# Feed-forward stages of a two-block transformer kernel: h's high and low parts in one 512-column product, halves added by VectorE

## The chip, the core and the metric

One Trainium2 chip, of which the program uses one core. The metric is the device time of one execution in microseconds (us); the table below has three runs. Names used: PE is TensorE, ACT is ScalarE, DVE is VectorE, POOL is GpSimd, SP is SyncE, whose queue issues the weight loads.

## The reference, cut to what matters

256 tokens of 1024 features pass six stages in float32: a gated MLP mixer, a feed-forward stage, an attention mixer, a second feed-forward stage, a gated linear attention mixer (GLA), and a convolutional feed-forward stage. Both plain feed-forward stages are

```python
h = modulate(rms_norm(x, norm_g[layer, 2]), sh2, sc2)               # 256 x 1024
y = jnp.square(jax.nn.relu(h @ ff_w_in[layer])) @ ff_w_out[layer]   # 1024 -> 4096 -> 1024
x = x + g2[:, None, :] * rms_norm(y, norm_g[layer, 3])
```

and the last stage is `u, gate = split(h @ w_up)`, a 3x3 convolution of `u` over a 4x64 grid, then `(silu(u) * gate) @ w_down` (1024 -> 2 x 2816 -> 1024). The modulation vectors (`sh`, `sc`, `g`) come from products of a condition vector with large matrices (`ada_w`), which are spread over the stages.

## The kernel before, in words

**Two-part products.** Each float32 factor is split into a high part (rounded to the matmul type, `fp32r`) and a low part (the rest). A product is the sum of three: high x high, high x low, low x high. For a weight chunk of 1 MB (a tile of 128 x 2048) ACT copies the raw tile to `whi` (L705, `hi`) and DVE writes `wlo = raw - whi` (L1174, `lo`). There are 6 raw slots and 3 slots of whi/wlo (`SPL`): `hi(m)` waits until PE has multiplied chunk m-3, `lo(m)` waits for `hi(m)`, PE waits for `lo(m)`. `hcat[:, kt, 0, :]` is the high part hh of the stage's input, `hcat[:, kt, 1, :]` the low part hl, each 256 tokens wide and side by side.

**A feed-forward stage** goes over 16 chunks c of 256 hidden features. PE's order is: ff_in(c+1), then rows(c). `ff_in(c)` (`linear_mid`, then `feature_major`) is 2 tiles of 128 features x 8 slices of h x 3 products of 256 columns (L1891 whi with hh, L1892 whi with hl, L1893 wlo with hh), 48 matmuls, all into one PSUM bank. `rows(c)` (`rows_onto_y`, L1959) multiplies the squares `fhi`, `flo` of chunk c (stationary) with the 512-column halves of the output weights, 24 matmuls. PSUM banks of ff_in rotate over 6, 4, 5.

**The step between them** (`epi(c)` in both `ffn` functions): ACT takes the relu out of PSUM to `fr` (L840) when ff_in(c) is done, then squares it into `fm` (L844); DVE squares `fr` into `fhi` (L1447) and subtracts, `flo = fm - fhi` (L1450). All 512 columns wide. Every engine runs its own list in program order. After epi(c), ACT does hi for the weights of rows(c) and of ff_in(c+2); DVE does lo for rows(c), then the condition products (next paragraph), then lo for ff_in(c+2).

**Condition products.** `FF_ADA[f][c]` says how many 1 MB chunks of ada_w are loaded and used at chunk c: 2,2,1,2,1,2,1,2,1,2,1,2,1,2,2,0 in the first stage, 2 and then fourteen 1 in the second. DVE multiplies and adds them (L1206 for 2048 columns; L1199 and L1202, a pair for a gate chunk); a batch of them ends with four matmuls that sum over the partitions (L1815) and its first one waits for the sum of the last batch of its kind.

**Other places that the change touches.** `oP` is the start of a region of the on-chip memory that each stage uses anew; `fhi`, `flo` and, in the last stage, `chi`, `clo` (the same parts of the gated activations, L1767 and L1772) lie in it. `GAIN_BANKS` names the PSUM banks for the gain rows (L1835). In attention, `rows_onto_y(M_BO[0])` is the first output product (two tiles of 128 tokens) and stands between head pair 7's two turns. In the last stage's last chunk, DVE does 4 of 8 convolution taps (L1755), lo of the last weight chunk, the other taps, waits for ACT's silu, then L1767, waits for ACT's `chi`, then L1772.

## Time and profile before

| what | value |
|---|---|
| median of 3 runs | 1033.72 us (1033.54 to 1035.16) |
| the profiled execution | 1034.27 us |
| its span, first to last instruction | 1032.5 us |
| granted TensorE clock, mean | 0.998 |
| PE matmul busy | 1005.6 us, 97% |
| DVE busy | 798.3 us, 77% |
| ACT busy | 537.9 us, 52% |
| HBM read | 239.37 MB |

The busy time of PE counts pipelined matmuls that overlap: a matmul of 256 columns is shown with 0.28 us, but the next one starts 0.12 us after it. What a matmul costs is read from the distance of the starts. The span's 1032.5 us leave 1.8 us of the profiled execution outside.

### The profile page before, as it was taken

To read this page: it belongs to the slowest core of one execution; us is meant where nothing else is said; L and a number is where in the kernel's file an instruction comes from. 1 tells how busy PE (TensorE), PEld (TensorE's weight loads), DVE (VectorE), ACT (ScalarE), POOL (GpSimd) and SP (SyncE) were. 2 spreads that over 40 slices of the span, in tenths; PEclk is the share of its full clock that TensorE was granted. 3 is DMA by queue.
4 is the path that set the end of the run, shared out by engine and by line. 5 is a ranking of instruction groups with operands and counts; after the bars stand their busy time and mean duration, and the time that the engine had idled before them with its cause. 6 is when DMAs were issued, how large, how long until landed. Compare 5 with 4: busy or idle time off the path is not lost.

```text
span 1032.5 us, 17024 instructions
## 1 busy us (share of the span) xinstructions
PE 1005.6 (97%) x6953; PEld 882.6 (85%) x6953; DVE 798.3 (77%) x1196; ACT 537.9 (52%) x706; POOL 76.2 (7%) x80
## 2 busy tenths in 40 slices
PE   6999999999999999999999999999999999999996
PEld 3687799888888999887989899898998789999995
DVE  2458798777988987867968778872796889878896
ACT  4353644445446457765545444455764565454543
POOL 0000000000000000000720000000890000000000
PEclk9999999999999999999999999999999999999999
DMA  9998699887997998003988787724344185656501
GB/s 340 387 391 334 232 339 360 310 333 263 357 327 258 287 369 317 2 2 124 391 305 322 260 289 281 245 78 136 124 163 160 46 285 205 199 169 203 167 39 42
DMA packets 130333, 243.62 MB, mean 236 GB/s; under 512 B 6586, under 2 KB 95311, under 8 KB 124111
## 3 DMA queue, kind: packets, MB, share of 16 engines
q1 hardware_dynamic: 125616, 238.77, 65.7%
q10 hardware_dynamic: 4639, 3.76, 1.3%
q8 instruction: 55, 0.90, 0.4%
q14 instruction: 23, 0.19, 0.1%
HBM read 239.37 MB, written 1.05 MB: 233 GB/s over the span
## 4 chain that ended last, share of the span: by engine, by line
PE 74%; DVE 11%; DMA 5%; SPq 3%; ACT 3%; issue 3%; DVEq 0%; ACTq 0%
PE bank L1959 21%; PE bank L1891 12%; PE bank L1893 12%; PE bank L1892 12%; DVE wlo L1174 3%; DMA raw<-in_a_w_in_dram 3%; SPq L635 2%; PE bank L1971 2%; PE bank L2244 1%; DMA raw<-in_b_w_in_dram 1%; PE bank L1847 1%; PE bank L1797 1%; PE bank L2270 1%; DMA raw<-in_ff_w_in_dram 1%; ACT whi L705 1%
## 5 line engine op out<-in xcount | busy, mean ns | idle before, releaser
L1174 DVE TENSOR_TENSOR wlo<-raw,whi 128x2048 fp32r<-128x2048 f32 x144 | 330.9, 2304 | 51.6 <-ACT whi L705 50.6
L705 ACT ACTIVATE whi<-raw 128x2048 fp32r<-128x2048 f32 x144 | 274.1, 1904 | 146.2 <-PE bank L1959 80.4
L1891 PE MATMUL bank<-hcat,whi 128*128 128x256 f32 x1096 | 312.5, 285 | 1.1 <-DVE wlo L1174 1.1
L1893 PE MATMUL bank<-hcat,wlo 128*128 128x256 f32 x1096 | 309.9, 283 | 0.0
L1892 PE MATMUL bank<-hcat,whi 128*128 128x256 f32 x1096 | 309.9, 283 | 0.0
L1891 PEld LDWEIGHTS bank<-hcat,whi 128*128 128x128 f32 x1096 | 209.8, 191 | 7.7 <-issue 3.0
L1892 PEld LDWEIGHTS bank<-hcat,whi 128*128 128x128 f32 x1096 | 209.9, 192 | 1.5
L1893 PEld LDWEIGHTS bank<-hcat,wlo 128*128 128x128 f32 x1096 | 209.9, 192 | 0.0
L1755 DVE SCALAR_TENSOR_TENSOR cvt<-ut,vec,cvt 128x189 f32<-128x189 f32 (+2 forms) x176 | 68.1, 429 | 21.0 <-ACT cvt L1137 18.6
L1959 PE MATMUL bank<-whi,fhi 128*128 128x512 f32 x240 | 76.5, 400 | 0.0
L1959 PE MATMUL bank<-whi,flo 128*128 128x512 f32 x240 | 75.4, 395 | 0.0
L1959 PE MATMUL bank<-wlo,fhi 128*128 128x512 f32 x240 | 74.9, 393 | 0.0
L840 ACT ACTIVATE fr<-bank 128x512 f32<-128x512 f32 x32 | 19.1, 598 | 90.6 <-PE bank L1893 84.5
L1206 DVE SCALAR_TENSOR_TENSOR acc_wide<-raw,csil,acc_wide 128x2048 f32<-128x2048 f32 x28 | 65.6, 2342 | 0.6
L1959 PEld LDWEIGHTS bank<-wlo,fhi 128*128 128x128 f32 x240 | 45.2, 188 | 10.8
L1959 PEld LDWEIGHTS bank<-whi,flo 128*128 128x128 f32 x240 | 45.0, 188 | 10.4
L1959 PEld LDWEIGHTS bank<-whi,fhi 128*128 128x128 f32 x240 | 43.3, 189 | 11.5 <-issue 3.4
L1447 DVE TENSOR_TENSOR fhi<-fr 128x512 fp32r<-128x512 f32 x32 | 22.4, 698 | 27.5 <-ACT fr L840 27.0
L1797 PE MATMUL bank<-raw,cpad 128*32 128x512 f32 x256 | 32.7, 627 | 6.5 <-DMA raw<-in_ada_w_dram 5.2
L786 ACT ACTIVATE t<-bank,mod,coef 128x256 f32<-128x256 f32 x64 | 30.4, 577 | 8.8 <-PE bank L1847 8.8
L1959 PE MATMUL bank<-whi,hcat 128*128 128x512 f32 x112 | 32.0, 394 | 1.4 <-DVE hcat L1734 1.4
L717 ACT ACTIVATE stage<-bank 128x512 f32<-128x512 f32 x15 | 9.1, 608 | 41.3 <-PE bank L1815 26.3
(425 smaller groups left out, 1651.1 us busy)
## 6 DMA issues: line engine op xcount, KB each, us to landing
raw<-in_ada_w_dram SPq DMA_DIRECT2D x40, 1024.0 KB, 8.3
raw<-in_ff_w_in_dram SPq DMA_DIRECT2D x32, 1024.0 KB, 7.2
raw<-in_ff_w_out_dram SPq DMA_DIRECT2D x32, 1024.0 KB, 6.9
raw<-in_w_ada_dram SPq DMA_DIRECT2D x24, 1024.0 KB, 6.2
raw<-in_w_up_dram SPq DMA_DIRECT2D x22, 1024.0 KB, 5.0
raw<-in_w_in_dram SPq DMA_DIRECT2D x12, 1024.0 KB, 5.4
raw<-in_w_down_dram SPq DMA_DIRECT2D x11, 1024.0 KB, 4.9
raw<-in_ada_w_dram SPq DMA_DIRECT2D x16, 512.0 KB, 12.2
```

Of the source, the lines that this page charges most:

```text
L635: sp.dma_start(raw[:, n % RAW, 0:k * w].rearrange("p (k n) -> p k n", n=w), s)\
L705: act.activation(whi[:, m % SPL, 0:w], raw[:, pl.nm[m] % RAW, 0:w], ACT.Copy).then_inc(s_hi, 1)
L786: act.activation(t32[:, kt, :], ps[banks[kt // 2]][:, T * (kt % 2):T * (kt % 2) + T], ACT.Identity, scale=coef[:, c, kt:kt + 1], bias=mod[ ...
L1174: dve.tensor_tensor(wlo[:, m % SPL, 0:w], raw[:, pl.nm[m] % RAW, 0:w], whi[:, m % SPL, 0:w], ALU.subtract).then_inc(s_lo, 1)
L1206: ins = dve.scalar_tensor_tensor(out=to[:, :], in0=w, scalar=s, in1=to[:, :], op0=ALU.mult, op1=ALU.add)
L1447: dve.tensor_tensor(fhi[:, c % 3, :], fr[:, :], fr[:, :], ALU.mult).then_inc(s_fh, 1)
L1755: ins = dve.scalar_tensor_tensor(out=y, in0=grid(ut)[:, frm[0], frm[1]], scalar=vec[:, w_:w_ + 1], in1=y, op0=ALU.mult, op1=ALU.add)
L1797: mm = pe.matmul(ps[ADA_BANK][32 * g:32 * g + 32, :], cpad[:, c, k, :], w, start=i == 0, stop=i == CHUNKS[b] - 1)
L1891: pe.matmul(dst, wh[:, kt, n], ah[:, kt, :], start=kt == 0, stop=False)
L1892: pe.matmul(dst, wh[:, kt, n], al[:, kt, :], start=False, stop=False)
L1893: mm = pe.matmul(dst, wl[:, kt, n], ah[:, kt, :], start=False, stop=kt == KT - 1)
L1959: mm = pe.matmul(ps[2 * t + half][:, :], st_, w[:, k, n[half]], start=first and k + i == 0, stop=False, skip_group_check=True)
```

## The change

For chunks 1 to 15 of both feed-forward stages, whi is multiplied with hh and hl side by side in one matmul of 512 columns, and wlo with hh in one of 256, into a bank for each tile of 128 features (so two banks a chunk, 31 turns of the rotation in place of 16). The bank's left half then holds two of the products and the right half the third. ACT copies the right half to `cb`, DVE adds the left half to it into `fr`, for each of the two tiles; when both are there ACT takes the relu from `fr` to `rl`, squares it to `fm`, and DVE's `fhi` is max(fr, 0) x fr. Chunk 0 keeps its products; DVE copies its bank to `fr`. `oP` moves by 128 bytes, so that it lies like `whi_at` modulo 512 bytes: `fhi`, `flo`, `chi`, `clo` start at 0 modulo 512 before and at 128 after, where `whi`, `wlo` and `hcat` are. `cv` of the GLA stage is at 384 before and after. The rest is the order of the last chunk's lo, the split of M_BO[0]'s product in attention, and the bank of a gain row.

```diff
--- before.py
+++ after.py
@@ -177,12 +177,12 @@
         pl.restart()
         win, wout = I["ff_w_in"][f], I["ff_w_out"][f]
         M_FF[f] = pl.m(cols(win, 0))
-        pl.m(cols(win, 256))
+        pl.m(cols(win, 256), 2)
         for c in range(16):
             pl.m(rows(wout, 2 * c), 0)
             ada_loads(FF_ADA[f][c])
             if c < 14:
-                pl.m(cols(win, 256 * (c + 2)))
+                pl.m(cols(win, 256 * (c + 2)), 2)
 
     if has("ffn0"):
         ffn_loads(0)
@@ -263,6 +263,7 @@
         return nc.alloc_sbuf_tensor_at(name, shape, dt, offset=take(size) if off is None else off)
 
     raw = sb("raw", [P, RAW, CH])
+    whi_at = at[0]
     whi = sb("whi", [P, SPL, CH], F32R)
     wlo = sb("wlo", [P, SPL, CH], F32R)
     x = sb("x", [P, 2, D])
@@ -308,7 +309,7 @@
     root = sb("root", [P, 2])
     dull = sb("dull", [P, 1])
     rsy = sb("rsy", [P, 2])
-    oP = place(at[0], 512)
+    oP = whi_at + (at[0] - whi_at + 511) // 512 * 512
     LIMIT = 229368
 
     acc = [sb("acc_wide", [P, 2048], F32, (LIMIT - 8192) // 128 * 128), sb("acc_gate", [P, 1024], F32, (LIMIT - 8192 - 4096) // 128 * 128)]
@@ -350,6 +351,8 @@
     r = region(oP, LIMIT)
     fr = r("fr", [P, 512])
     fm = r("fm", [P, 512])
+    rl = sb("rl", [P, 512], F32, oS + 20480)
+    cb = sb("cb", [P, 2, T], F32, oS + 22528)
     fhi = r("fhi", [P, 3, 512], F32R)
     flo = r("flo", [P, 3, 512], F32R)
 
@@ -508,6 +511,7 @@
     s_lv, s_lr, s_vn = sem("v_variance_ready"), sem("v_rsqrt_guess"), sem("v_normed")
     s_wsT, s_wTc, s_wT = sem("ws_transposed"), sem("ws_copied"), sem("ws_masked")
     s_mix, s_oa = sem("mixed"), sem("gmlp_out_split")
+    s_fu, s_rl, s_cb = sem("ffn_first_features_multiplied"), sem("ffn_relu_ready"), sem("ffn_low_halves_copied")
     s_fsq, s_fh, s_fact = sem("ffn_squared"), sem("ffn_hi"), sem("ffn_act_ready")
     s_out = sem("out_stored")
     s_ht, s_htT = sem("cmp_hidden_rows"), sem("cmp_hidden_transposed")
@@ -544,7 +548,7 @@
     U_GMLP, U_FF0, U_ATT, U_FF1, U_GLA, U_FF2 = range(6)
     N_UPD = [0, 1, 2, 3, 4, 5, 6][stage_n]
 
-    GAIN_BANKS = {U_GMLP: (5, 6), U_FF0: (6, 4), U_ATT: (6, 6), U_FF1: (6, 4), U_GLA: (4, 5), U_FF2: (7, 5)}
+    GAIN_BANKS = {U_GMLP: (5, 6), U_FF0: (5, 4), U_ATT: (6, 6), U_FF1: (5, 4), U_GLA: (4, 5), U_FF2: (7, 5)}
 
 
     CTX_STEPS = (9, 10, 11, 12)
@@ -832,16 +836,19 @@
                 m0, c0 = M_FF[f], 16 * f
                 u0 = pl.um[m0]
                 def epi(c):
-                    m = m0 + (2 * c - 1 if c else 0)
-                    act.wait_ge(s_mm, m + 1)
-                    if c0 + c > 0:
-                        act.wait_ge(s_fh, c0 + c)
-                        act.wait_ge(s_fsq, c0 + c)
-                    act.activation(fr[:, :], ps[pl.bank[u0 + c]][:, :], ACT.Relu).then_inc(s_mid, 1)
-                    act.wait_ge(s_mid, u0 + c + 1)
+                    for k in range(2 if c else 0):
+                        if k:
+                            act.wait_ge(s_mm, m0 + 2 * c)
+                        else:
+                            act.wait_ge(s_fu, 15 * f + c)
+                        act.wait_ge(s_mid, u0 + max(2 * c - 2 + k, 1))
+                        act.activation(cb[:, k, :], ps[pl.bank[u0 + 2 * c - 1 + k]][:, T:2 * T], ACT.Copy).then_inc(s_cb, 1)
+                    act.wait_ge(s_mid, u0 + 2 * c + 1)
+                    act.activation(rl[:, :], fr[:, :], ACT.Relu).then_inc(s_rl, 1)
+                    act.wait_ge(s_rl, c0 + c + 1)
                     if c0 + c > 0:
                         act.wait_ge(s_fact, c0 + c)
-                    act.activation(fm[:, :], fr[:, :], ACT.Square).then_inc(s_fsq, 1)
+                    act.activation(fm[:, :], rl[:, :], ACT.Square).then_inc(s_fsq, 1)
 
                 for c in range(16):
                     epi(c)
@@ -1173,6 +1180,12 @@
                     return
                 dve.tensor_tensor(wlo[:, m % SPL, 0:w], raw[:, pl.nm[m] % RAW, 0:w], whi[:, m % SPL, 0:w],
                                   ALU.subtract).then_inc(s_lo, 1)
+
+            def lo_half(m, i):
+                if i == 0:
+                    dve.wait_ge(s_hi, m + 1)
+                n = slice(1024 * i, 1024 * i + 1024)
+                return dve.tensor_tensor(wlo[:, m % SPL, n], raw[:, pl.nm[m] % RAW, n], whi[:, m % SPL, n], ALU.subtract)
 
             macs = [0]
             next_load = [0]
@@ -1440,11 +1453,20 @@
                 m0, c0 = M_FF[f], 16 * f
                 mid0 = pl.um[m0]
                 def epi(c):
-                    dve.wait_ge(s_mid, mid0 + c + 1)
+                    if c0 + c > 0:
+                        dve.wait_ge(s_rl, c0 + c)
+                    if c == 0:
+                        dve.wait_ge(s_mm, m0 + 1)
+                        dve.tensor_copy(fr[:, :], ps[pl.bank[mid0]][:, :]).then_inc(s_mid, 1)
+                    for k in range(2 if c else 0):
+                        dve.wait_ge(s_cb, 30 * f + 2 * c - 1 + k)
+                        dve.tensor_tensor(fr[:, T * k:T * k + T], ps[pl.bank[mid0 + 2 * c - 1 + k]][:, 0:T], cb[:, k, :], ALU.add).then_inc(s_mid, 1)
+                    dve.wait_ge(s_mid, mid0 + 2 * c + 1)
                     if c >= 3:
 
                         dve.wait_ge(s_mm, m0 + 2 * (c - 3) + 3)
-                    dve.tensor_tensor(fhi[:, c % 3, :], fr[:, :], fr[:, :], ALU.mult).then_inc(s_fh, 1)
+                    dve.scalar_tensor_tensor(out=fhi[:, c % 3, :], in0=fr[:, :], scalar=0.0, in1=fr[:, :],
+                                             op0=ALU.max, op1=ALU.mult).then_inc(s_fh, 1)
                     dve.wait_ge(s_fh, c0 + c + 1)
                     dve.wait_ge(s_fsq, c0 + c + 1)
                     dve.tensor_tensor(flo[:, c % 3, :], fm[:, :], fhi[:, c % 3, :], ALU.subtract).then_inc(s_fact, 1)
@@ -1756,17 +1778,22 @@
                                                            op0=ALU.mult, op1=ALU.add)
                         ins.then_inc(s_tap, 1)
                         dve.wait_ge(s_tap, 8 * c + n + 1)
-                        if n == 3:
-                            splits((M_UP[c + 1] if c + 1 < CF else M_DN[c]) + 1)
+                        if n == 3 and c + 1 < CF:
+                            splits(M_UP[c + 1] + 1)
                     if c + 1 < CF:
                         splits(M_GA[c + 1] + 1)
+                    else:
+                        lo_half(M_DN[c], 0)
                     dve.wait_ge(s_mm, M_GA[c] + 1)
                     dve.wait_ge(s_sil, c + 1)
                     if c:
                         dve.wait_ge(s_cact, c)
                     dve.tensor_tensor(fa[:, :, :], sl[:, :, :], ps[4 + c % 2][:, :].rearrange("p (k t) -> p k t", t=T), ALU.mult)\
                        .then_inc(s_fa, 1)
-                    splits(M_DN[c] + 1)
+                    if c + 1 < CF:
+                        splits(M_DN[c] + 1)
+                    else:
+                        lo_half(M_DN[c], 1).then_inc(s_lo, 1)
                     dve.wait_ge(s_fa, c + 1)
                     dve.wait_ge(s_chi, c + 1)
                     dve.tensor_tensor(clo[:, c % 2, :], fa[:, :, :].rearrange("p k t -> p (k t)"), chi[:, c % 2, :], ALU.subtract)\
@@ -2003,7 +2030,20 @@
                 m0, c0 = M_FF[f], 16 * f
                 u0 = pl.um[m0]
                 def ff_in(c, o=None):
-                    linear_mid(m0 + (2 * c - 1 if c else 0), hh, hl, o=o)
+                    if c == 0:
+                        linear_mid(m0, hh, hl, o=o)
+                        return
+                    m = m0 + 2 * c - 1
+                    split_ready(m)
+                    wh, wl = w_of(m)
+                    for nt in range(2):
+                        mid_free(u0 + 2 * c - 1 + nt)
+                        bank, n = ps[pl.bank[u0 + 2 * c - 1 + nt]], slice(P * nt, P * nt + P)
+                        for kt in range(KT):
+                            pe.matmul(bank[:, :], wh[:, kt, n], hcat[:, kt, :, :].rearrange("p s t -> p (s t)"),
+                                      start=kt == 0, stop=False, skip_group_check=True)
+                            mm = pe.matmul(bank[:, 0:T], wl[:, kt, n], hh[:, kt, :], start=False, stop=kt == KT - 1, skip_group_check=True)
+                        mm.then_inc(s_mm if nt else s_fu, 1)
 
                 def squares(c):
                     pe.wait_ge(s_fact, c0 + c + 1)
@@ -2025,7 +2065,7 @@
                         ctx_transposes(CTX_STEPS.index(c + 1))
                     if c >= 13:
 
-                        pe.wait_ge(s_mid, u0 + c)
+                        pe.wait_ge(s_mid, u0 + 2 * c + 1)
                         gain_row(u, c - 13)
                     if c < 14:
                         rows_onto_y(m0 + 2 * c + 2, *squares(c), first=c == 0)
@@ -2299,7 +2339,8 @@
                     else:
 
                         pe.wait_ge(s_Sev, NH)
-                        rows_onto_y(M_BO[0], *h_rows(0), first=True)
+                        split_ready(M_BO[0])
+                        tile_onto_y(M_BO[0], *h_rows(0), 0, True)
                     turn(2 * p + 1)
                     if p == 0:
 
@@ -2307,6 +2348,7 @@
                         ada_bank_free(S1B)
                         pe.wait_ge(s_one, 3)
                     values(2 * p)
+                tile_onto_y(M_BO[0], *h_rows(0), 1, True).then_inc(s_mm, 1)
                 values(NH - 1)
 
                 def last_pair(p):
```

## Rows read from the trace of the kernel before

**Rows 1.** The profile's first part: busy time, share of the span, instructions.

```profile
PE 1005.6 (97%) x6953; PEld 882.6 (85%) x6953; DVE 798.3 (77%) x1196; ACT 537.9 (52%) x706; POOL 76.2 (7%) x80
```

**Rows 2.** Waits in the first feed-forward stage, 132 to 308 us: total, times, longest.

```profile
DVE fhi L1447 <- ACT fr L840: 15.2, 7, 6.8
...
PEld bank L1891 <- DVE wlo L1174: 0.4, 1, 0.4
```

**Rows 3.** Timeline of PE at chunk 5: start, us, engine, line, operation, count.

```profile
178.00 0.28 PE L1891 MATMUL bank<-hcat,whi 128*128 128x256 f32 x1
...
183.63 0.28 PE L1893 MATMUL bank<-hcat,wlo 128*128 128x256 f32 x1
183.75 0.62 PE L1959 MATMUL bank<-whi,fhi 128*128 128x512 f32 x2
...
189.32 0.28 PE L1891 MATMUL bank<-hcat,whi 128*128 128x256 f32 x1
```

**Rows 4.** Timeline of PE in attention, 18 matmuls with hcat stationary.

```profile
454.16 1.08 PE L1959 MATMUL bank<-whi,hcat 128*128 128x512 f32 x4
...
458.25 0.62 PE L1959 MATMUL bank<-whi,hcat 128*128 128x512 f32 x2
```

**Rows 5.** Timeline of ACT at chunk 5 of the first feed-forward stage.

```profile
183.95 0.60 ACT L840 ACTIVATE fr<-bank 128x512 f32<-128x512 f32 x1 [3.77 <-PE bank L1893]
184.58 0.63 ACT L844 ACTIVATE fm<-fr 128x512 f32<-128x512 f32 x1
185.12 1.90 ACT L705 ACTIVATE whi<-raw 128x2048 fp32r<-128x2048 f32 x1
```

**Rows 6.** Timeline of DVE at chunk 5, with two gate chunks.

```profile
184.58 0.69 DVE L1447 TENSOR_TENSOR fhi<-fr 128x512 fp32r<-128x512 f32 x1 [2.07 <-ACT fr L840]
...
187.05 2.29 DVE L1174 TENSOR_TENSOR wlo<-raw,whi 128x2048 fp32r<-128x2048 f32 x1 [1.04 <-ACT whi L705]
189.26 0.74 DVE L1201 TENSOR_SCALAR acc_gate<-raw,csil 128x1024 f32<-128x1024 f32 x1
...
193.95 2.28 DVE L1174 TENSOR_TENSOR wlo<-raw,whi 128x2048 fp32r<-128x2048 f32 x1
```

**Rows 7.** Timeline of DVE at chunk 10, where it is behind PE.

```profile
251.79 2.35 DVE L1206 SCALAR_TENSOR_TENSOR acc_wide<-raw,csil,acc_wide 128x2048 f32<-128x2048 f32 x1
254.05 2.29 DVE L1174 TENSOR_TENSOR wlo<-raw,whi 128x2048 fp32r<-128x2048 f32 x1
256.25 0.68 DVE L1447 TENSOR_TENSOR fhi<-fr 128x512 fp32r<-128x512 f32 x1
```

**Rows 8.** Lines 1585 (DVE) and 976 (ACT), from PSUM: ns min/median/max, starts.

```profile
L1585 DVE TENSOR_TENSOR hcat<-bank,hcat x2: 417/421/425, 469.1 to 470.1; 128x256 fp32r<-128x256 f32 x2
L976 ACT ACTIVATE hcat<-bank x2: 384/384/385, 463.7 to 469.7; 128x256 fp32r<-128x256 f32 x2
```

**Rows 9.** Timeline of DVE: chunk 1 and chunk 15 of the first feed-forward stage.

```profile
141.83 0.69 DVE L1447 TENSOR_TENSOR fhi<-fr 128x512 fp32r<-128x512 f32 x1
...
305.36 0.69 DVE L1450 TENSOR_TENSOR flo<-fm,fhi 128x512 fp32r<-128x512 f32 x1
```

**Rows 10.** Timelines of DVE, chunks 1 and 15 of the second stage, and PE after.

```profile
508.27 0.69 DVE L1447 TENSOR_TENSOR fhi<-fr 128x512 fp32r<-128x512 f32 x1
...
668.65 0.69 DVE L1450 TENSOR_TENSOR flo<-fm,fhi 128x512 fp32r<-128x512 f32 x1
...
670.43 1.06 PE L1815 MATMUL bank<-acc_wide,one 128*32 128x512 f32 x8
```

**Rows 11.** Timelines of DVE and PE at the last chunk of the last stage.

```profile
1017.66 0.69 DVE L1767 TENSOR_TENSOR fa<-sl,bank 128x512 f32<-128x512 f32 x1 [0.87 <-ACT sl L1144]
1017.73 1.09 PE L1835 MATMUL bank<-diag,oner 128*128 128x512 f32 x4
...
1019.11 0.69 DVE L1772 TENSOR_TENSOR clo<-fa,chi 128x512 fp32r<-128x512 f32 x1 [0.77 <-ACT chi L1147]
...
1019.86 0.50 PE L1971 MATMUL bank<-whi,chi 128*128 128x512 f32 x1 [1.04 <-DVE clo L1772]
```

## The prediction

> **What bounds the kernel now.** I read the engines' shares first: PE is busy 97% of the span, DVE 77%, ACT 52% [rows 1]. Then the waits of the first feed-forward stage: PE waits for a converted weight once, 0.4 us in all [rows 2]; DVE has slack, 15.2 us of waiting for ACT's relu at 7 of 16 chunks. Then PE's timeline at chunk 5 [rows 3]: ff_in runs from 178.00 to 183.75 (48 matmuls of 256 columns in 5.75 us, 0.120 each), rows from 183.75 to 189.32 (24 of 512 columns in 5.57 us, 0.232 each). A chunk is 11.32 us, back to back. So PE sets the time as long as DVE and ACT deliver within 11.32 us a chunk. That is the question for this change, which takes work from PE and gives work to the other two.
>
> **1. The merged product, on PE.** In attention 18 matmuls of 512 columns with hcat stationary take 4.09 us, 0.227 each [rows 4]. One of 512 in place of two of 256 saves 0.240 - 0.227 = 0.013 us; 30 chunks x 2 tiles x 8 slices = 480 pairs give 6.4 us. No row has hcat moving at 512 columns; if it costs the 0.232 of rows 3 it is 3.8 us. I take 6.4, the hcat row.
>
> The Trainium skill, "TensorE: Matmul & The Clock Gate", section "Back-to-back issue gap", gives a start-to-start distance of columns / 2.4 GHz plus 2.5 ns; by it the merge would save 480 x 2.5 ns = 1.2 us. Rows 3 and 4 show about 13 ns over the columns' time, so the trace speaks against the page here.
>
> **2. The place of fhi, flo, chi, clo.** Same shape, same moving operand: 0.232 us with fhi (0 modulo 512) and 0.227 us with hcat (128 modulo 512) stationary [rows 3, 4]. After the change fhi lies like hcat. 768 matmuls in the two stages would save 0.005 each, 3.9 us, 264 in the last stage 1.3 us. Lower bound nothing (two tensors are a thin case); I take the rows.
>
> PE's chunk becomes 16 x (0.227 + 0.120) + 24 x 0.227 = 11.0 us.
>
> **3. The step between, on ACT and DVE.** Before, in steady state: relu 183.95, square 184.58, next hi 185.12 [rows 5], all needing only PE and DVE's previous chunk. So when DVE was late, ACT's hi for rows(c) was ready long before DVE came to its lo. After, ACT's relu needs both of DVE's adds of the same chunk, and hi stands behind relu and square in ACT's order. So after DVE's adds it must wait a whole ACT conversion:
> - adds: two of 128x256 with a PSUM operand at 0.42 [rows 8], the second a little overlapped, and the signal: 0.84 us. The copies at 0.38 [rows 8] lie beside.
> - relu 0.63 and square 0.54 to the start of hi, hi 1.90 and the signal: 3.10 us [rows 5]; DVE's fhi and flo (1.4 us) lie inside this, and DVE idles for the rest.
> - lo for rows(c) 2.20, lo for ff_in(c+2) 2.20 [rows 7], taken as 4.42 with their signals.
>
> That is 8.36 us a chunk plus the condition products: 2.27 for a wide one (251.79 to 254.05) [rows 7], 2.35 each for two gate chunks with the first of a batch (189.26 to 193.95) [rows 6], 2.6 for a later one. Before, a chunk cost DVE 1.3 + 4.4 = 5.7 plus the same. With one product DVE's chunk is now 10.6 us, with two 12.9; the first stage alternates 1 and 2, on average 11.8 against PE's 11.0. In the second stage it is 10.6 to 11.0 against 11.0, on the edge. A price between: nothing, if DVE never falls behind, up to the whole chain.
>
> **4. First stage, DVE's chain end to end.** DVE enters chunk 1 at 141.83 before [rows 9]; chunk 0's bank copy and the longer wait for the square add 1.3: 143.1. From there: 14 x 8.36 = 117.0; condition products of chunks 1 to 14, six wide (13.6), four gate (10.0), eight wide (17.3), four gate (10.0) = 50.9; gain diagonals 2.8, three modulations 1.1, ACT's gain copy ahead of a hi 0.6, a wait behind ACT's DMA issues 0.5; last step 2.8. Sum 175.7, end 318.8. Before, flo of chunk 15 ended at 305.36 + 0.69 = 306.05 [rows 9]: 12.8 us later. PE waits for exactly this flo before its four sum matmuls, in both kernels. PE's 14 x 0.3 us saved are inside: it only waits longer. Its stalls should be small up to chunk 13 (0.3 to 1.3 us, while the 3 weight slots and DVE's lead are used up), then some 3.5 us at ff_in(15), which waits for a gain row that ACT copies after the relu of chunk 14, and 6 us ahead of the sum.
>
> **5. Second stage.** Entry 508.27 + 1.3 = 509.6 [rows 10]; 117.0 + products 32.6 + the context's norm, splits and gate weights on DVE 9.9 + diagonals 2.8 + slowed stretch beside POOL 1.5 + small ones 4.6 = 168.4 (terms without a row of their own, here and in 4, are read from DVE's timeline of the stage), so 678.0 against 668.65 + 0.69 = 669.34. PE came to its sum only at 670.43 [rows 10], so the end moves by 7.6.
>
> The same count with before's durations ends 0.8 and 0.5 us ahead of the trace; I add this 1.3.
>
> **6. The last stage and its end.** PE is the bound there: 264 x 0.005 = -1.3 us. In the last chunk DVE now does its taps without the 2.2 us lo between; the halves (1.15 each) lie in its waits for silu and chi (0.87 and 0.77) [rows 11]. clo starts 2.2 + 0.87 + 0.77 - 2 x 1.1 = 1.6 us earlier, so PE, which is through with its four gain matmuls at 1017.73 + 4 x 0.23 = 1018.65 and goes on at 1019.86 [rows 11], goes on at once: -1.2 us.
>
> **7. Edits costed at nothing.** M_BO[0]'s split moves 2.8 us of PE work behind values(14); the total is the same and PE has no gap there (rows 4 stand in it), at most 0.3 either way. Without that cover the later release of a weight slot would hold up hi for M_BO[3]. The gain bank and the rotation over 31 turns: a bank is needed again after 11 us, while DVE is at most 8 late; the cover goes where it is later. SP's loads are issued later, when lo frees a slot, as DVE is; it now takes longer over each, so they land in time. The first product of each stage is unchanged.
>
> **Sum** against the profiled execution: +12.8 + 7.6 + 1.3 - 36 x 2 x 0.005 (0.4, the stages' last matmuls) - 1.3 - 1.2 = +18.8; 1034.27 + 18.8 = 1053.1. The median stands 0.55 below the profiled execution: 1052.5 us, 1.8% slower.
>
> **Rivals.**
> - A, forecast, 0.71: DVE and ACT's chain sets both stages. With copies, adds, relu and square some tenth cheaper or dearer, my count moves by -6 and +5: 1046.5 to 1057.5.
> - B, 0.18: the chain binds in the first stage only, as the second is on the edge; there only the end of the stage is late, +3, and the first gives +8. With -2.5 of the last stage: 1042. For it: 10.6 against 11.0. Against: context work comes on top in chunks 5 to 12.
> - C, the other side, 0.09: DVE keeps its lead and PE stays the bound. Then -6.4 - 3.9 - 1.3 - 1.2 = -12.8, so 1021. It decides at the price of the step: the first stage has room for 11.0 - 9.2 = 1.8 us a chunk over before (5.7 + 3.5), and I count 2.66. For it: 15.2 us of slack [rows 2]. Against: 2.66 x 14 = 37 us, more than twice that slack.
> - D, 0.02: B's mild form and PE's savings cancel, within 0.2%, about what a measurement can tell here.
> - Inside A and B: the place gives nothing. Then the feed-forward stages don't change, as PE isn't their bound, and the last loses its 1.3: 1053.8.
>
> The Trainium skill, "SBUF — State Buffer", section "Specifications (TRN2)", speaks of cachelines of 16 bytes; 0 and 128 modulo 512 are both whole ones, so by that rule this last case holds. The difference of rows 3 and 4 speaks against it; I give the rule 1 in 5.
>
> **Range and chances.** 1042 to 1058 holds A and most of B. Faster 0.09 (C), same 0.02 (D), slower 0.89.
>
> **What would show it.** Right: in the changed kernel's first feed-forward stage, relu waits for DVE's add and DVE's lo for ACT's hi (1.1 us at nearly each chunk), a chunk takes PE 11.6 to 11.9 us on average, and PE waits about 6 us for the last flo; lower PE share, higher DVE share; 0.347 us for a pair of 512 and 256 columns; L1959 with fhi at 0.227; no wait of PE behind L1835 at the end. Wrong: DVE waits for PE's ff_in at most chunks (C), or PE's chunk in the second stage is 11.0 to 11.1 us to the end (B).

## The result, and the profile after

The changed kernel takes 1056.33 us (median, 1052.67 to 1056.81), the kernel before 1034.44 beside it: ratio 1.0206, 95% interval 1.0185 to 1.0227, so 2.1% slower. The profiled execution took 1056.81 us, its span is 1055.1 against 1032.5. Forecast were 1052.5 us and a range of 1042 to 1058. Of five executions of one experiment (work in place of the waits) one took 1655.17 us at a mean clock of 0.557; it is left out of that experiment's time and ratio.

The page's first part, of the changed kernel:

```profile
PE 1009.7 (96%) x6473; PEld 861.0 (82%) x6473; DVE 820.5 (78%) x1259; ACT 555.7 (53%) x766; POOL 70.6 (7%) x80
```

Against [rows 1] PE has 480 instructions less and is busy *longer*; DVE has 22 us more work. I cut both spans at PE's first transposition of x in each stage, and the last stage at PE's last matmul. Lengths in the profiled executions, before and after, in us:

| stage | before | after | difference |
|---|---|---|---|
| first feed-forward | 195.5 | 209.0 | +13.5 |
| attention | 167.0 | 168.8 | +1.8 |
| second feed-forward | 197.3 | 206.4 | +9.1 |
| linear attention | 146.4 | 146.5 | +0.1 |
| last | 198.6 | 196.0 | -2.6 |

Two waits of the whole changed kernel (total, times, longest):

```profile
ACT rl L847 <- DVE fr L1463: 133.7, 30, 7.7
DVE wlo L1181 <- ACT whi L709: 58.8, 45, 6.1
```

ACT's relu now waits for DVE's adds in all 30 chunks that have them. Before, it was DVE that waited for the relu [rows 2]. The roles have turned round: DVE is behind from the first chunks on. Its timeline over one chunk of the first stage, with one condition product in it (the line ahead is the start of the chunk before, which has two):

```profile
143.19 0.75 DVE L1463 TENSOR_TENSOR fr<-bank,cb 128x256 f32<-128x256 f32 x2
...
156.25 0.75 DVE L1463 TENSOR_TENSOR fr<-bank,cb 128x256 f32<-128x256 f32 x2
157.03 0.69 DVE L1468 SCALAR_TENSOR_TENSOR fhi<-fr 128x512 fp32r<-128x512 f32 x1
158.43 0.69 DVE L1472 TENSOR_TENSOR flo<-fm,fhi 128x512 fp32r<-128x512 f32 x1 [0.71 <-ACT fm L851]
160.17 2.29 DVE L1181 TENSOR_TENSOR wlo<-raw,whi 128x2048 fp32r<-128x2048 f32 x1 [1.04 <-ACT whi L709]
162.38 2.35 DVE L1219 SCALAR_TENSOR_TENSOR acc_wide<-raw,csil,acc_wide 128x2048 f32<-128x2048 f32 x1
164.64 2.29 DVE L1181 TENSOR_TENSOR wlo<-raw,whi 128x2048 fp32r<-128x2048 f32 x1
166.84 0.75 DVE L1463 TENSOR_TENSOR fr<-bank,cb 128x256 f32<-128x256 f32 x2
```

and ACT's beside it:

```profile
157.03 0.63 ACT L847 ACTIVATE rl<-fr 128x512 f32<-128x512 f32 x1 [7.07 <-DVE fr L1463]
157.70 0.63 ACT L851 ACTIVATE fm<-rl 128x512 f32<-128x512 f32 x1
158.24 3.70 ACT L709 ACTIVATE whi<-raw 128x2048 fp32r<-128x2048 f32 x2
```

ACT stands idle for 7.07 us, then makes relu, square and conversion while DVE waits 0.71 and 1.04 us for them. The chunk takes 10.59 us (156.25 to 166.84), the one before it with two products 13.06 (143.19 to 156.25). So each of the two waits for the other in turn, and neither is busy all through: what binds is the round that they make together. The low squares (flo) of chunk 15 end the stage. DVE's of both stages, and PE at the end of the first:

```profile
317.93 0.69 DVE L1472 TENSOR_TENSOR flo<-fm,fhi 128x512 fp32r<-128x512 f32 x1 [0.70 <-ACT fm L851]
...
693.18 0.69 DVE L1472 TENSOR_TENSOR flo<-fm,fhi 128x512 fp32r<-128x512 f32 x1 [0.70 <-ACT fm L851]
```

```profile
318.68 1.50 PE L1842 MATMUL bank<-acc_gate,one 128*32 128x512 f32 x4 [4.11 <-DVE flo L1472]
...
320.71 0.63 PE L1998 MATMUL bank<-wlo,fhi 128*128 128x512 f32 x1
321.13 0.63 PE L1998 MATMUL bank<-whi,flo 128*128 128x512 f32 x1
...
322.72 0.40 PE L1998 MATMUL bank<-whi,fhi 128*128 128x512 f32 x1
322.95 0.40 PE L1998 MATMUL bank<-wlo,fhi 128*128 128x512 f32 x1
```

PE waits 4.1 us for it. And there is something that my sum has no term for: behind the wait the matmuls of 512 columns start 0.42 us apart (320.71 and 321.13), and from 322.72 on 0.23. Busy time by stretch shows why (columns: stretch, its length; PE, PEld, DVE, ACT and POOL busy; PE's granted clock; DMA share; GB/s):

```profile
305.50:308.90 3.40, 3.40 (x12) 2.92 (x12) 3.19 (x2) 2.35 (x3) 0.00 (x0) 0.50 0.62 255
319.10:322.50 3.40, 3.40 (x10) 1.91 (x7) 2.29 (x1) 1.61 (x2) 0.00 (x0) 0.51 0.42 145
445.40:448.80 3.40, 3.40 (x18) 2.82 (x18) 2.27 (x6) 1.98 (x5) 0.00 (x0) 0.51 0.00 0
616.10:619.50 3.40, 3.40 (x10) 2.85 (x11) 2.19 (x5) 2.50 (x3) 0.00 (x0) 0.50 0.93 307
694.60:698.00 3.40, 3.40 (x11) 2.24 (x8) 2.29 (x1) 1.30 (x2) 0.00 (x0) 0.50 0.79 244
```

Five times the granted clock is at its lower level, 1.2 GHz, for 3.4 us, though PE is busy all through. Four of them stand behind a wait of PE (3.1, 4.1, 2.4 and 2.2 us) and begin 0.0 to 1.6 us after its end; the third stands in attention, where PE had not been idle. The profiled execution of the kernel before shows none between 15 us and PE's last matmul.

### The profile page after: what moved, and what is told of

It is laid out like the page before. It is cut to its first block, busy times and chain, and to the rows that moved or that the text cites. A ratio compares the mean times of both kernels' runs of the same rounds, so it can differ in the third digit from the quotient of the medians.

```text
span 1055.1 us, 16245 instructions
## 1 busy us (share of the span) xinstructions
PE 1009.7 (96%) x6473; PEld 861.0 (82%) x6473; DVE 820.5 (78%) x1259; ACT 555.7 (53%) x766; POOL 70.6 (7%) x80
## 4 chain that ended last, share of the span: by engine, by line
PE 61%; DVE 18%; ACT 8%; issue 7%; DMA 4%; SPq 2%; DVEq 0%; ACTq 0%
PE bank L1986 16%; PE bank L1918 7%; PE bank L1919 7%; PE bank L1920 7%; DVE wlo L1181 6%; ACT whi L709 4%; PE bank L2043 4%; DVE acc_wide L1219 3%; DMA raw<-in_a_w_in_dram 3%; PE bank L1998 2%; PE bank L2045 2%; PE bank L2284 1%; PE bank L1824 1%; PE bank L2310 1%; ACT rl L847 1%
## 5 line engine op out<-in xcount | busy, mean ns | idle before, releaser
L2043 PE MATMUL bank<-hcat,whi 128*128 128x512 f32 x480 | 173.5, 403 | 7.8 <-ACT gain L727 4.5
L1918 PE MATMUL bank<-hcat,whi 128*128 128x256 f32 x616 | 176.0, 286 | 1.1 <-DVE wlo L1181 1.1
L1919 PE MATMUL bank<-hcat,whi 128*128 128x256 f32 x616 | 174.3, 283 | 0.0
L1918 PEld LDWEIGHTS bank<-hcat,whi 128*128 128x128 f32 x616 | 118.1, 192 | 6.4 <-issue 3.0
L1919 PEld LDWEIGHTS bank<-hcat,whi 128*128 128x128 f32 x616 | 118.1, 192 | 0.4
L2043 PEld LDWEIGHTS bank<-hcat,whi 128*128 128x128 f32 x480 | 90.9, 189 | 32.9 <-DVE wlo L1181 6.0
L847 ACT ACTIVATE rl<-fr 128x512 f32<-128x512 f32 x32 | 20.3, 633 | 142.6 <-DVE fr L1463 133.7
L1472 DVE TENSOR_TENSOR flo<-fm,fhi 128x512 fp32r<-128x512 f32 x32 | 22.2, 693 | 22.5 <-ACT fm L851 22.5
## 6 DMA issues: line engine op xcount, KB each, us to landing
raw<-in_ada_w_dram SPq DMA_DIRECT2D x16, 512.0 KB, 12.1
```

What stands on the lines that cost most here:

```text
L847: act.activation(rl[:, :], fr[:, :], ACT.Relu).then_inc(s_rl, 1)
L1472: dve.tensor_tensor(flo[:, c % 3, :], fm[:, :], fhi[:, c % 3, :], ALU.subtract).then_inc(s_fact, 1)
L1918: pe.matmul(dst, wh[:, kt, n], ah[:, kt, :], start=kt == 0, stop=False)
L1919: pe.matmul(dst, wh[:, kt, n], al[:, kt, :], start=False, stop=False)
L2043: pe.matmul(bank[:, :], wh[:, kt, n], hcat[:, kt, :, :].rearrange("p s t -> p (s t)"), start=kt == 0, stop=False, skip_group_check=True)
```

## The experiments

**The theory:** the chain from DVE's adds through ACT's relu, square and conversion to DVE's lo sets the length of both feed-forward stages. **Rivals:** DVE's added busy time by itself (1); the merged product or its rotation of two banks costs PE the time (2). Times are medians, ratios go against the kernel before, run beside each.

### The merge taken back

```diff
-                pl.m(cols(win, 256 * (c + 2)), 2)
+                pl.m(cols(win, 256 * (c + 2)))
```

and with it the first pl.m(cols(win, 256)), ff_in, both epi and the gain banks as in the kernel before.

> The changed kernel with both feed-forward stages as before (48 products of 256 columns a chunk, ACT's relu straight from the bank, one bank a chunk, the old gain bank); fhi, flo, chi, clo stay at their new place, and the last chunk's halves and the attention split stay. Theory (the chain of DVE's adds, ACT's relu, square and conversion, DVE's lo costs the time): 1034.4 - 5.2 (place) - 1.2 (end) = 1028. If the place gives nothing: 1033. Rival (attention's split or the place itself costs, not the step): 1040 or more, with attention still 1.8 us longer than before.

1029.68 us, ratio 0.9948 (0.9930 to 0.9966); the stages take 193.4, 167.1, 195.6, 146.4 and 196.0 us. All that was lost lies in the merge with its step; the new place, the last chunk's halves and the attention split together are a gain of some 5.5 us. Attention is at its old length, so the split did not make it longer.

### Only the products merged, and only the step

First the products alone, with ACT and DVE as before and one relu of the chunk's second bank:

```diff
-                    act.activation(rl[:, :], fr[:, :], ACT.Relu).then_inc(s_rl, 1)
+                    act.activation(fr[:, :], ps[pl.bank[u0 + 2 * c]][:, :], ACT.Relu).then_inc(s_mid, 2 if c else 1)
```

> The changed kernel with the merged products and two banks a chunk, but ACT and DVE as before: one relu of the second bank's 512 columns, no copies, no adds, relu and square in the old order. It leaves out the sum of high and low halves and the first tile's half of the chunk. Theory: PE is the bound again, with a pair at 0.354 us against 0.360 for three: 1034.4 - 2.9 - 5.2 - 1.2 = 1025, and PE without waits over 1 us in the stages. Rival 2 (merged product or its banks cost the time): 1050 or more. Rival 1 and the theory agree here.

Then the step as in the change, and the product in two of 256 columns:

```diff
-                            pe.matmul(bank[:, :], wh[:, kt, n], hcat[:, kt, :, :]..., start=kt == 0, ...)
+                            pe.matmul(bank[:, 0:T], wh[:, kt, n], hh[:, kt, :], start=kt == 0, ...)
+                            pe.matmul(bank[:, T:2 * T], wh[:, kt, n], hl[:, kt, :], start=False, ...)
```

> The changed kernel with its whole new step on ACT and DVE (copies, adds, relu, multiply with max, square) and its banks, but PE makes the high and the low part of h in two products of 256 columns instead of one of 512. Theory: PE has slack in the first stage, so its 2.9 us more are hidden there and half seen in the second: 1056 to 1059. Rival 2 (the merged product costs the time): 1028 to 1035. If the four stretches of half clock behind PE's waits matter, they are here again, as the waits are.

Products alone: 1027.50 us, ratio 0.9925 (0.9907 to 0.9943), stages of 191.9 and 194.0 us, no wait of PE over 1 us in them. Step alone: 1054.43 us, ratio 1.0189 (1.0173 to 1.0206), stages of 209.1 and 203.5. Rival 2 falls: the step costs the time without the merge, and the merge costs nothing without the step. DVE's chunk in the step alone, over the same stretch, is that of the changed kernel to 0.01 us:

```profile
155.83 0.75 DVE L1463 TENSOR_TENSOR fr<-bank,cb 128x256 f32<-128x256 f32 x2
...
159.74 2.29 DVE L1181 TENSOR_TENSOR wlo<-raw,whi 128x2048 fp32r<-128x2048 f32 x1 [1.04 <-ACT whi L709]
...
166.41 0.74 DVE L1463 TENSOR_TENSOR fr<-bank,cb 128x256 f32<-128x256 f32 x2
```

Against the merge taken back (193.4 and 195.6), the products alone save 1.5 + 1.6 = 3.1 us, 0.0065 for each of 480 pairs. In the changed kernel a pair takes 0.353 us, start to start (the mean of 430 pairs that follow each other at the upper clock), against 0.360 for three of 256 columns, as in these rows (304.38 to 304.73):

```profile
304.38 0.39 PE L2043 MATMUL bank<-hcat,whi 128*128 128x512 f32 x1
304.61 0.28 PE L2045 MATMUL bank<-hcat,wlo 128*128 128x256 f32 x1
304.73 0.40 PE L2043 MATMUL bank<-hcat,whi 128*128 128x512 f32 x1
```

### The conversion ahead of the relu

ACT's hi for rows(c) needs only that ff_in(c) has ended, and DVE's lateness leaves ACT idle just then.

```diff
                         act.activation(cb[:, k, :], ..., ACT.Copy).then_inc(s_cb, 1)
+                    if c:
+                        splits(m0 + 2 * c + 3)
                     act.wait_ge(s_mid, u0 + 2 * c + 1)
                     act.activation(rl[:, :], fr[:, :], ACT.Relu).then_inc(s_rl, 1)
```

> The changed kernel, but ACT converts the weights of rows(c) ahead of the relu of chunk c and not behind its square; nothing is added or left out. Theory: DVE's wait of 1.04 us for that conversion goes from nearly every chunk; its chunk falls from 10.6 and 12.9 to 9.6 and 11.9 us, 10.8 on average against PE's 11.1, so PE is about the bound again: 1036 to 1044, and the waits of lo for the conversion fall from 59 us to under 30. Rival 1 (DVE's added busy time alone, whatever its order): under 4 us less, 1052 to 1056. Rival 2 (the merged product or its two banks cost PE the time): 1056, unchanged.

1038.74 us, ratio 1.0038 (1.0025 to 1.0051); stages of 199.8 and 197.2. A move of one instruction on ACT, with no work less anywhere, gives back 17.6 of 21.9 us. Part of that is the clock's: its profile has two stretches of half clock ahead of PE's last matmul, where the changed kernel's has five. DVE's chunk of one product:

```profile
154.68 0.75 DVE L1465 TENSOR_TENSOR fr<-bank,cb 128x256 f32<-128x256 f32 x2
...
156.86 0.69 DVE L1474 TENSOR_TENSOR flo<-fm,fhi 128x512 fp32r<-128x512 f32 x1 [0.70 <-ACT fm L853]
157.47 2.29 DVE L1183 TENSOR_TENSOR wlo<-raw,whi 128x2048 fp32r<-128x2048 f32 x1
...
164.13 0.75 DVE L1465 TENSOR_TENSOR fr<-bank,cb 128x256 f32<-128x256 f32 x2
```

The wait of 1.04 us is gone, the chunk is 9.45 us and not 10.59. DVE is busy for 818.3 us, as long as before this edit (820.5): rival 1 falls too. Of the conversion waits I expected under 30 us in all: 23.9.

### The low squares behind the lo, with and without that

```diff
                                              op0=ALU.max, op1=ALU.mult).then_inc(s_fh, 1)
+                    splits(m0 + min(2 * c + 3, 33))
                     dve.wait_ge(s_fh, c0 + c + 1)
                     dve.wait_ge(s_fsq, c0 + c + 1)
```

Together with the conversion ahead:

> The version with the conversion ahead of the relu, and besides that DVE makes the lo of the weights of rows(c) between the chunk's high squares and its low squares; nothing is left out. Theory (the order of the coupled steps, not DVE's busy time): DVE's last wait in the step, 0.7 us for the square, goes too, its chunk falls from 9.4 and 11.9 us to 8.7 and 11.2, 9.9 on average against PE's 11.1, so PE is the bound nearly throughout: the first stage 192 to 195 us, the second 194 to 196, and 1027 to 1032 in all. Rival 1 (DVE's added busy time): as with the conversion first alone, 1037 to 1040, since DVE's work is the same. Rival 3 (the low squares are now later by 2.3 us, so PE waits for them): 1040 or more, with a wait behind flo at each chunk.

1034.44 us, ratio 0.9995 (0.9985 to 1.0005): the miss is 2 us above the range. The mechanism came as expected: the chunk is 8.67 us (153.93 to 162.60), without any wait:

```profile
153.93 0.75 DVE L1465 TENSOR_TENSOR fr<-bank,cb 128x256 f32<-128x256 f32 x2
...
155.32 2.28 DVE L1183 TENSOR_TENSOR wlo<-raw,whi 128x2048 fp32r<-128x2048 f32 x1
157.53 0.68 DVE L1475 TENSOR_TENSOR flo<-fm,fhi 128x512 fp32r<-128x512 f32 x1
...
162.60 0.74 DVE L1465 TENSOR_TENSOR fr<-bank,cb 128x256 f32<-128x256 f32 x2
```

But PE still waited 2.8 and 2.0 us for the last low squares, with half clock behind both. In chunk 15 the lo that now stands ahead of them is of the next stage's weights (302.00), and nobody waits for it there:

```profile
302.00 2.28 DVE L1183 TENSOR_TENSOR wlo<-raw,whi 128x2048 fp32r<-128x2048 f32 x1
304.20 0.69 DVE L1475 TENSOR_TENSOR flo<-fm,fhi 128x512 fp32r<-128x512 f32 x1
```

The same edit alone, with ACT's order as in the change:

> The changed kernel with one part of the good order alone: DVE makes the lo of rows(c)'s weights ahead of the low squares, while ACT still converts those weights behind relu and square. Theory (the chain from DVE's adds through ACT's relu, square and conversion to the lo): nothing on that chain gets shorter, DVE now waits 1.7 us at the lo and not 0.7 and 1.0 at two places, and the low squares, which lay inside the wait, come on top: 8.36 + 0.69 = 9.05 us a chunk and product time, slower than the changed kernel by 0.65 us for each of some 26 chunks in which DVE binds, and 2.2 us at each stage's end: 1070 to 1078. Rival 4 (it was the low squares' wait for the square that cost the time): 1040 to 1048, 0.7 us less a chunk. Rival 1 (DVE's busy time): 1056, unchanged.

1083.05 us, ratio 1.0463 (1.0446 to 1.0481), the slowest of all, though of the same work. DVE's chunk is 11.20 us (156.93 to 168.13):

```profile
156.93 0.75 DVE L1463 TENSOR_TENSOR fr<-bank,cb 128x256 f32<-128x256 f32 x2
...
160.85 2.29 DVE L1181 TENSOR_TENSOR wlo<-raw,whi 128x2048 fp32r<-128x2048 f32 x1 [2.44 <-ACT whi L709]
...
168.13 0.75 DVE L1463 TENSOR_TENSOR fr<-bank,cb 128x256 f32<-128x256 f32 x2
```

0.61 us more a chunk, as expected (0.65): the low squares had been free inside the wait. The whole is 5 us above my range. I had set 2.2 us for a stage's end, but there a wait for the conversion joins the lo, about 4 us (the profile shows PE waits of 9.2 and 5.8 us at the two ends), and PE's clock is at its lower level seven times, for 34 us in all; how the 5 us divide between the two was not measured.

### The last chunk left as it was

```diff
-                    if c:
+                    if 0 < c < 15:
                         splits(m0 + 2 * c + 3)
-                    splits(m0 + min(2 * c + 3, 33))
+                    if c < 15:
+                        splits(m0 + 2 * c + 3)
```

> The version with the conversion ahead of the relu and the low squares behind the lo, but in the last chunk of a stage both stand as in the changed kernel, since the weights that they convert there belong to the next stage. Theory: the low squares of chunk 15 come 2.2 us earlier, PE's last waits of 3.0 and 2.2 us fall to under 1 us, and the half clock behind them (1.4 to 1.7 us each) goes with them: 1034.4 - 2.1 - 1.4 - 2 x 1.5 = 1028, below the kernel before (1034.9), near the version without the merge (1029.7). If the half clock isn't tied to these waits: 1031. If next stage's weights then come late: a new wait of 2 us at the start of the attention stage, 1032 or more.

1028.44 us, ratio 0.9938 (0.9925 to 0.9950), where 1028 was expected; stages of 192.5 and 194.8 us. PE in the first stage, ahead of the sum:

```profile
303.24 1.05 PE L1846 MATMUL bank<-acc_gate,one 128*32 128x512 f32 x4 [1.24 <-DVE flo L1476]
```

The wait is 1.24 us and not 4.11, the clock stays at its upper level there, and no new wait came at the start of attention (one of 1.6 us, 62 us into it, stands in the version with the products alone too, with 1.5). This version does all the work of the changed kernel, is 27.9 us faster, and is 0.6% faster than the kernel before. Against the merge taken back (0.9948, 0.9930 to 0.9966) its lead can't be told from nothing. Its two stages are 0.9 and 0.8 us shorter than there, and the products alone saved 3.1 us: well ordered, the merge is worth no more than that.

### The small edits alone, on the kernel before

```diff
-    oP = place(at[0], 512)
+    oP = whi_at + (at[0] - whi_at + 511) // 512 * 512
```

> The kernel before, with fhi, flo, chi and clo moved from 0 to 128 modulo 512 bytes and nothing else. If the place decides the time of a product with its stationary operand there: 0.227 us instead of 0.232, 3.8 us less in the two feed-forward stages and 1.3 in the last: 1029.2, ratio 0.995. If it does nothing: ratio 1.000, and the products stay at 0.232.

1031.54 us, ratio 0.9970 (0.9958 to 0.9981). The products with fhi, flo, chi and clo start 0.227 us apart and not 0.232, and the three stages take 193.4, 195.7 and 197.5 us: 2.1 + 1.6 + 1.1 = 4.8 less, near the 5.1 expected. But attention takes 169.5 us and not 167.0, with a 3.4 us stretch of half clock in it, so that the ratio lies between my two cases.

```diff
-                    splits(M_DN[c] + 1)
+                    if c + 1 < CF:
+                        splits(M_DN[c] + 1)
+                    else:
+                        lo_half(M_DN[c], 1).then_inc(s_lo, 1)
```

> The kernel before, with the last chunk's low weights made in two halves behind the taps and nothing else. Theory: the last wait of PE for clo, 1.2 us, goes, ratio 0.9988. Rival: the time is taken back by whatever PE or DVE waits for next: ratio 1.000.

1033.37 us, ratio 0.9988 (0.9979 to 0.9997), just as expected; PE's last stage is 197.2 and not 198.6 us.

```diff
-                        rows_onto_y(M_BO[0], *h_rows(0), first=True)
+                        split_ready(M_BO[0])
+                        tile_onto_y(M_BO[0], *h_rows(0), 0, True)
...
+                tile_onto_y(M_BO[0], *h_rows(0), 1, True).then_inc(s_mm, 1)
                 values(NH - 1)
```

> The kernel before, with M_BO[0]'s product in two parts, the second behind the last values but one, and nothing else. As I costed it: nothing, ratio 1.000 (0.9995 to 1.0005). If the split is worth what was lost at the start of the output products: 0.999. If the 3.4 us of half clock that the attention stage shows in most of the variants comes with the split: attention 169 us and not 167, ratio 1.002.

1033.77 us, ratio 0.9995 (0.9986 to 1.0005): nothing, as costed.

### Work in place of the waits

```diff
                 def squares_ready():
+                    ada_bank_free(ends_at(f, 14))
+                    keep_warm(18 if f == 0 else 10, ADA_BANK)
                     pe.wait_ge(s_fact, c0 + 16)
```

> The changed kernel, and PE runs products of zeros into the idle bank of the condition sums (18 of 512 columns in the first stage, 10 in the second, some 4.0 and 2.2 us) ahead of its wait for the last low squares, inside the 4.3 and 2.4 us that it waits there anyway; the result is not touched. If the 3.4 us stretches of half clock come from PE's idle time just before: the two behind these waits go and the matmuls of 512 columns behind them take 0.227 and not 0.43 us, 1 to 1.7 us less each, 1053 to 1054.5 in all; the stretches behind the waits at 305 and 616 us stay. If they come from something else: they stay and the time is 1056 or, where the products run over the wait, 0.5 us more.

1054.13 us, ratio 1.0188 (1.0174 to 1.0202), which can't be told from the changed kernel's (1.0206, 1.0185 to 1.0227); what can be read is the one profile. In the second stage the products filled the wait, no stretch of half clock stands behind it, and the stage takes 204.9 and not 206.4 us. PE there, and its clock over 692 to 695 us:

```profile
691.48 2.11 PE L1867 MATMUL bank<-zb 128*128 128x512 bf16 x9
```

```profile
692.00:695.00 3.00, 2.90 (x17) 0.95 (x16) 0.93 (x2) 2.97 (x4) 0.00 (x0) 1.00 1.10 352
```

In the first stage they came too late: the bank was read only at 315 us, PE stood idle for 2.7 us all the same, and the half clock fell on the products of zeros:

```profile
315.37 5.52 PE L1867 MATMUL bank<-zb 128*128 128x512 bf16 x17 [2.71 <-DVE mod L1365]
320.82 1.05 PE L1842 MATMUL bank<-acc_gate,one 128*32 128x512 f32 x4
...
322.14 0.40 PE L1998 MATMUL bank<-wlo,fhi 128*128 128x512 f32 x1
322.38 0.39 PE L1998 MATMUL bank<-whi,flo 128*128 128x512 f32 x1
```

The half clock came right behind the idle 2.7 us, now ahead of the real work, which then ran at 0.23 us. As the 18 products (17 of them recorded) took 5.5 us and not 4, they overran the wait and the stage gained nothing (210.0 against 209.0).

Of the two stretches that were expected to stay, the one at 616 us stayed (615.9). The one at 305 us did not, though nothing had been put in its place and PE waited 3.14 us there:

```profile
303.50 0.50 PE L2043 MATMUL bank<-hcat,whi 128*128 128x512 f32 x1 [3.14 <-ACT gain L727]
```

```profile
305.50:308.90 3.40, 3.40 (x21) 2.93 (x20) 3.37 (x3) 1.82 (x2) 0.00 (x0) 1.00 0.77 253
```

The step alone gives a second such case, at the very wait that was filled here. There PE waits 2.15 us at the end of the second stage with nothing in its place, and the products behind it start 0.24 us apart:

```profile
692.40 1.07 PE L1842 MATMUL bank<-acc_wide,one 128*32 128x512 f32 x8 [2.15 <-DVE flo L1472]
...
693.98 0.40 PE L1998 MATMUL bank<-whi,flo 128*128 128x512 f32 x1
694.22 0.40 PE L1998 MATMUL bank<-whi,fhi 128*128 128x512 f32 x1
```

So this run doesn't show that the products in the wait prevented the half clock: it can be missing without them. That it comes from the idle time fits most rows, and is not proven.

## Why the prediction was right

**Forecast A, the chain in both stages, is what happened.** Relu waits for DVE's adds, lo for the conversion (1.04 us, forecast 1.1), PE for the last low squares; the rows are above.

**Steps 3 and 4.** Forecast was a chunk of 10.6 and 12.9 us; measured 10.59 and 13.06 (12.1 to 14.4 over the first stage's eight chunks with two). The terms that the sum adds to that fit as well: from chunk 1's adds to chunk 15's DVE took 172.6 us in the first stage and 165.6 in the second, where steps 4 and 5 without their last step of 2.8 give 172.9 and 165.6. PE's chunk up to ff_in(14) was 11.9 us on average, at the upper end of the 11.6 to 11.9 named. The last low squares of the first stage were forecast to end at 318.8 us and ended at 318.62. The wait at ff_in(15) was forecast as 3.5 us and was 3.1; ahead of the sum 6 were forecast and 4.1 came. Between these two waits PE ran at half clock for 3.4 us (305.50 to 308.90), which made its own work some 1.7 us longer and its wait as much shorter. So that stretch cost the stage nothing.

**Step 5.** From stage start, the last low squares were forecast 8.66 us later than before. They ended at 693.87, 24.53 after 669.34 [rows 10]; less the 13.5 + 0.5 of the stages ahead and attention's 1.8 that is 8.7. The context work did come on top, as A had it against B.

**Step 1 was mis-sized.** "One of 512 in place of two of 256 saves 0.240 - 0.227 = 0.013 us", 6.4 us in all: measured are 0.0065 a pair and 3.1 us; a pair takes 0.353 us, where 0.347 was named as a sign. I took the price of a run of equal matmuls from [rows 4] for one that alternates with matmuls of 256 columns. It cost the forecast nothing, as PE was not the bound; had C come, 1021 would have been 3 us too low by this term (the products alone, C's case without the step, took 1027.50). The 1.2 us that the Trainium skill's rule for a matmul by itself ("TensorE: Matmul & The Clock Gate", section "Back-to-back issue gap") gives is too little as well: the measurement lies between the two.

**Step 2 was right.** 0.227 in place of 0.232 us, and 4.8 us less in three stages with that edit alone. So the size of the cacheline, from the Trainium skill's "SBUF — State Buffer", section "Specifications (TRN2)", does not decide this: places that are both whole cachelines differ. What does decide it is open; only these two places were tried.

**Steps 6 and 7.** Last stage -2.6 us (forecast -2.5); the split worth nothing; the gain bank and the rotation harmless (the products merged alone had no wait from them).

**What the sum lacks.** Forecast +18.8, measured +22.6 between the spans. The prediction has no term for PE's clock. The ends of the two stages run at half clock: 1.5 us more between the last low squares and the next stage in the first (11.4 against 9.9), 1.5 in the second by the stage's +9.1 against 7.6. Attention is 1.8 longer, with a stretch in it. That is 4.8, against which stand the 1.3 us by which I corrected my count and which were not needed. The rest, 0.3 us, is small terms. The range had 5 us of room above the forecast for dearer copies, adds, relu and square; those came as priced, and it was the clock that used up most of the room. That the time still lay inside is luck in this respect.

**Of the rivals,** C put the point of decision at 1.8 us a chunk over before, whose chunk with one product is 8.0 (5.7 + 2.27). At 8.67 us, 0.7 over, PE is nearly always the bound. At 9.45, 1.5 over and still below C's point, the first stage takes 199.8 us, of which PE waits 4.0 at its end: the average room of a chunk leaves out the other work of DVE in the stage and its last step. B was wrong at the edge it named: in the second stage DVE's 14 chunks took 165.6 us, where 14 of PE's 11.1 are 155.

## What to carry to other kernels

Whether additions can move off a full engine onto one with slack was decided here by the order in which the two helpers serve each other, not by their busy shares: the same instructions took 1083, 1056, 1039, 1034 or 1028 us by their order alone, the half clock behind the longer waits included. Follow one chunk round the ring (who waits for whom, and what stands ahead of it in that engine's order), put ahead of a wait what depends on nothing in it, and treat the last round apart, where the work that was brought forward belongs to the next stage. What was free inside a wait is not free once it is moved out of it.

## What the runs showed of the hardware

**Half clock behind a wait.** In the changed kernel PE's granted clock fell to its lower level for 3.4 us within 1.6 us behind waits of 3.1, 4.1, 2.4 and 2.2 us, and matmuls of 512 columns took 0.43 us apart in place of 0.23. So a wait on PE can cost more than its length: 1.5 us at each stage's end here, and at most 1.7 by the estimate of half a stretch. Not every wait has one behind it. Behind a wait of 3.14 us (work in place of the waits), of 2.15 us (the step alone) and of 1.96 us (the slowest experiment) none stood, behind waits of 2.0 and 1.8 us (both orders together) one did, and behind those of 1.2 to 1.7 us none in any profile. What tells them apart stays open, and the length alone doesn't.

**The kernel's start is slow too.** The clock column reads 1.00 there, but its records begin only at 12.6 to 15.4 us, and by the pace of the matmuls PE is at about half of it until then. In the kernel before, eight products of the same line and shape took 1.94 us behind PE's first waits and 1.06 from 15.7 us on:

```profile
6.52 1.94 PE L1797 MATMUL bank<-raw,cpad 128*32 128x512 f32 x8 [3.61 <-DMA raw<-in_ada_w_dram]
...
18.72 1.07 PE L1797 MATMUL bank<-raw,cpad 128*32 128x512 f32 x8
```

**Half clock without a wait.** A stretch of the same length stood in attention where PE is busy without a break (in the changed kernel on matmuls of 65 to 272 columns), in the profiled executions of nine of the eleven experiments and of the changed kernel, not in that of the kernel before. In the profiles that have no other stretch in attention, the stage is 0.9 to 2.5 us longer than before. It is no part of any edit. Of the split alone's executions five had a mean clock of 0.999 and took 1033.4 us on average, five had 0.997 and took 1035.0; of the 22 of the kernel before that ran beside the later experiments, six had 0.999 and took 1033.7, eight had 0.997 and took 1035.0. One stretch lowers the mean by 3.4 x 0.5 / 1033 = 0.0016, so most of the spread between executions of one kernel may be one stretch more or less. What sets it off was not found, and no run was made for it.

**512 and 256 columns in turn** take 0.353 us, 0.006 more than the 0.227 and 0.120 that each takes among its like.

**The place of a stationary operand** at 0 or at 128 modulo 512 bytes makes 0.232 or 0.227 us of a matmul of 512 columns.
